# S5 responses beside the q, k, v products, S5 input tables beside the output projection, memory keys and values kept in SBUF

## The reference, cut to what matters

```python
for i in range(DEPTH):
    h = rms_norm(x, norm_w[i])
    if i % 2 == 0: seq_out, z, xq = gla_branch(h, ...)      # q, k, v, r, z, xq = h @ w_in
    else:          seq_out, z, xq = s5_branch(h, ...)       # x_t = Ab x_{t-1} + Bb u_t ; y_t = Re(C x_t)
    xa = memory_attention(xq, mem_n, xa_w_kv[i])
    x = x + (concatenate([seq_out, xa]) * silu(z)) @ w_out[i]
```

## Time and profile before

| | |
|---|---|
| median of 3 runs | 3059.97 us (3059.89 to 3063.43) |
| the profiled execution, its time | 3060.32 us |
| its span on the core | 3058.5 us |
| PE busy | 2840.8 us (93%) |
| DVE, ACT, POOL busy | 1407.5, 997.1, 1110.8 us |
| mean granted TensorE clock | 0.971 of full speed |
| DMA | 324.88 MB, mean 106 GB/s |

### The profile page before, as it was taken

The page is one execution under the profiler, slowest core; times in us unless marked ns, Lnnn a source line. Parts: engine busy times, 40 slices in busy tenths (PEclk is TensorE's granted clock), DMA queues, the critical chain, the costliest instruction groups (busy, mean ns, idle before and its releaser), DMA issues.

```text
span 3058.5 us, 45007 instructions
## 1 busy us (share of the span) xinstructions
PE 2840.8 (93%) x17982; PEld 2335.4 (76%) x17982; DVE 1407.5 (46%) x2200; ACT 997.1 (33%) x1525; POOL 1110.8 (36%) x780
## 2 busy tenths in 40 slices
PE   7998889899999999899989888899998999899997
PEld 5676567678788578787768877899997877678885
DVE  7688364510206611402138675570634456382452
ACT  2222444222312235523225333412124455332211
POOL 1332022444233179443433423244442321244442
PEclk9999999999999999999999998999999998999999
DMA  5888111145573279322221100222222210122222
GB/s 182 248 266 257 58 42 49 63 153 158 158 216 103 97 176 257 112 96 90 90 88 64 43 3 23 70 90 90 91 91 75 81 45 22 56 89 96 91 95 76
DMA packets 130815, 324.88 MB, mean 106 GB/s; under 512 B 54144, under 2 KB 54784, under 8 KB 129872
## 3 DMA queue, kind: packets, MB, share of 16 engines
q1 hardware_dynamic: 96272, 222.95, 22.8%
q0 software_dynamic: 30016, 87.92, 10.2%
q10 hardware_dynamic: 4352, 11.50, 1.0%
HBM read 288.32 MB, written 33.95 MB: 105 GB/s over the span
## 4 chain that ended last, share of the span: by engine, by line
PE 70%; DVE 16%; ACT 4%; DMA 3%; issue 3%; POOL 3%; DVEq 1%; ACTq 0%; SPq 0%; POOLq 0%
PE ps L270 17%; PE ps L273 17%; PE ps L275 17%; DMA d_pb<-arena 3%; POOL ring_r L363 2%; PE ps L280 2%; PE ps L925 1%; PE ps L1876 1%; PE ps L1615 1%; ACT high L372 1%; DVE h L603 1%; PE ps L1707 1%; PE ps L2291 1%; PE ps L3003 1%; DVE x L600 1%
## 5 line engine op out<-in xcount | busy, mean ns | idle before, releaser
L363 POOL TENSOR_TENSOR ring_r<-ring,high 128x1024 fp32r<-128x1024 f32 x335 | 834.4, 2491 | 1388.7 <-ACT high L372 1388.7
L270 PE MATMUL ps<-h_hi,high 128*128 128x512 f32 (+1 forms) x2104 | 735.4, 358 | 46.1 <-POOL ring_r L363 27.2
L275 PE MATMUL ps<-h_hi,ring_r 128*128 128x512 f32 (+1 forms) x2104 | 661.6, 349 | 0.0
L372 ACT ACTIVATE high<-ring 128x1024 fp32r<-128x1024 f32 x367 | 387.8, 1057 | 831.1 <-PE ps L270 695.7
L273 PE MATMUL ps<-h_r,high 128*128 128x512 f32 (+1 forms) x1912 | 642.9, 346 | 0.0
L270 PEld LDWEIGHTS ps<-h_hi,high 128*128 128x128 f32 x2104 | 400.1, 190 | 120.9 <-issue 48.3
L275 PEld LDWEIGHTS ps<-h_hi,ring_r 128*128 128x128 f32 x2104 | 370.0, 190 | 53.8
L273 PEld LDWEIGHTS ps<-h_r,high 128*128 128x128 f32 x1912 | 364.2, 190 | 41.9 <-issue 1.4
L273 PE MATMUL ps<-f_r,high 128*128 128x264 f32 (+1 forms) x960 | 295.1, 321 | 0.0
L270 PE MATMUL ps<-f_hi,high 128*128 128x264 f32 (+1 forms) x896 | 270.9, 317 | 2.2 <-POOL ring_r L363 1.7
L275 PE MATMUL ps<-f_hi,ring_r 128*128 128x264 f32 (+1 forms) x896 | 230.8, 316 | 0.0
(11 more groups left out here) (489 smaller groups left out, 4254.6 us busy)
## 6 DMA issues: line engine op xcount, KB each, us to landing
ring<-in_units SPq DMA_DIRECT2D x402, 512.0 KB, 3.3
d_ca<-arena POOLq DMA_DIRECT2D x16, 640.0 KB, 9.1
arena<-d_ca POOLq DMA_DIRECT2D x16, 640.0 KB, 6.0
arena<-d_q POOLq DMA_DIRECT2D x32, 256.0 KB, 8.0
d_pb<-arena POOLq DMA_DIRECT2D x16, 512.0 KB, 11.2
arena<-d_pb POOLq DMA_DIRECT2D x16, 512.0 KB, 4.0
arena<-d_ca POOLq DMA_DIRECT2D x16, 512.0 KB, 5.2
arena<-d_k POOLq DMA_DIRECT2D x128, 64.0 KB, 4.3
```

The lines of the kernel that those rows point to most:

```text
L270: part = mm(acc, hi[:, cols], self.x_hi(k)[:, t0:t0 + tn], start=(k == 0), stop=False)
L275: ins = mm(acc, w[:, cols], self.x_hi(k)[:, t0:t0 + tn], start=False, stop=(k == self.kt - 1))
L363: eng.tensor_tensor(b.ring_r[:, slot, :], b.ring[:, slot, :], self.high[:, (j + self.flip) % 2, :], ALU.subtract).then_inc(b.unit_lo, 1)
L372: b.nc.scalar.activation(self.high[:, (j + self.flip) % 2, :], b.ring[:, u % RING, :], ACT.Copy).then_inc(b.unit_hi, 1)
```

## The change

What each edit does:

- In xq, q, k, v, PE computes the responses of block n right after the second of the block's two units (`unit_tensor`, `respond`), from the `ca` in SBUF: 8 products with 32 weight columns (16 lag columns that nobody uses, and the 16 of Bb), each group written to one of four bands of 32 PSUM partitions. ACT keeps them (`keep_response`) after the high part of the unit two later, POOL stores them by 4 DMAs a block. POOL now loads only `cin` and `bin` for a block, stores 128 of the 160 columns of `ca`, and no `pb`. DVE makes no `pb` there. The loops over xq, q, k, v are written out.
- In `out0`, `S5InputTables` takes the place of `S5Responses`: DVE makes `pb` for two blocks ahead of each tile's add, POOL issues for each block a load of `bk` (512 KB), two loads of powers (`d_q`, 256 KB each) and a store of `pb` (512 KB). PE has only the projection.
- The memory's keys and values stay in SBUF; their two stores and two loads are gone.
- The norm of layer 1 also waits until the `pb` stores have landed; the next memory keys wait for nothing of the responses.

```diff
@@ S5Tables @@
+    def respond(self, pe, n):
+        b, m, par = self.b, self.m, n % 2
+        pe.wait_ge(self.made, n + 1)
+        if n >= 2:
+            pe.wait_ge(self.k_kept, n - 1)
+        for g in range(8):
+            i, j = divmod(g, QUARTERS)
+            ins = b.nc.tensor.matmul(b.ps[32 * j:32 * j + 32, 4 + 2 * par, i * P:(i + 1) * P],
+                                     m.ca[par][:, g, P:P + 32], m.ca[par][:, g, 0:P], start=True, stop=True)
+        ins.then_inc(self.responded, 1)
...
             if not isinstance(it, int) or it > 0:
-                dve.wait_ge(self.block_out[par], it * 32)
+                dve.wait_ge(self.block_out[par], it * 16)
+                dve.wait_ge(self.responded, m_ - 1)
...
-            inner(tt(bb, bb, small, ALU.add))
-            q, k = m.qk[par], m.bk[par]
-            t512 = m.tmp[:, 0:512]
...
-            inner(tt(t512, q[:, 1], k[0], ALU.mult))
-            tt(pbv[:, 1], pbv[:, 1], eight(t512), ALU.add).then_inc(self.made, 1)
+            tt(bb, bb, small, ALU.add).then_inc(self.made, 1)
@@ class S5InputTables(Stage) @@
+        def load(n):
+            par = n % 2
+            pool.dma_start(m.bk[par], a["s5_bk"][n].unsqueeze(0).broadcast_to([S5_C, S5_H, 2, 512])
+                           ).then_inc(self.block_in[par], 16)
+            q = b.d_q.rearrange("c k (m n) -> m k c n", m=NB)[n]
+            for c in range(2):
+                pool.dma_start(m.qk[par][:, c], q[:, c].unsqueeze(1).broadcast_to([S5_C, S5_H, 512])
+                               ).then_inc(self.block_in[par], 16)
...
+        def store(n):
+            pool.wait_ge(self.made, NB + n + 1)
+            pool.dma_start(b.d_pb[n], m.pb_made[n % 2]).then_inc(self.stored[n % 2], 16)
 
         load(0)
         load(1)
         for o in range(KD):
             for u in range(3 * o + 1, 3 * o + 4):
                 gemm.low_unit(pool, u)
                 if u == 3 * o + 1 and o:
                     for n in (2 * o - 2, 2 * o - 1):
                         store(n)
                         load(n + 2)
...
+    def scalar(self, act):
+        for o in range(KD):
+            for u in range(3 * o + 1, 3 * o + 4):
+                gemm.high_unit(act, u)
+            gemm.out_scalar(act, o)
...
+    def vector(self, dve):
+        b, gemm = self.b, self.beside
+        for o in range(KD):
+            self.block(dve, 2 * o)
+            self.block(dve, 2 * o + 1)
+            it, i = divmod(o, gemm.body_outs)
+            par, full = gemm.count(i, it)
+            dve.wait_ge(b.filled[par], full)
+            gemm.store("dve", o, gemm.bank(o), o).then_inc(b.stored[par], 1)
+            if o >= 2:
+                self.norm.add(dve, o - 1)
...
-        stages.append(LoadMemory())
+        stages.append(S5LastResponse(tables))
```

More of the change, by code:

```diff
@@ L178, in loop @@
     def loop(self, eng, body):
-        if self.squared_by or self.high is None and self.then or self.high is not None and (self.iters == 2 or self.after or self.before):
+        if self.aside or self.squared_by or self.high is None and self.then or self.high is not None and (self.iters == 2 or self.after or self.before):
             for it in range(self.iters):
@@ L1291, in __init__ @@
         self.beside = []
-        self.done = [(self.block_out[c], 32 * NB // 2) for c in range(2)]
+        self.cleared = b.sem("s5t_cleared")
+        self.responded = b.sem("s5t_responded")
+        self.k_kept = b.sem("s5t_k_kept")
+        self.k_stored = [b.sem("s5t_k_even"), b.sem("s5t_k_odd")]
+        self.done = [(self.block_out[c], 16 * NB // 2) for c in range(2)]
+        self.done += [(self.k_stored[c], 16 * QUARTERS * NB // 2) for c in range(2)]
     def load(self, pool, m_, par):
@@ L1298, in load @@
         pool.dma_start(m.bin[par], a["s5_ba"][m_]).then_inc(s, 16)
[L1299 to L1304, removed]
+    LOADS, INNER = 2, 5
     def store_powers(self, pool):
@@ L1602, in tensor @@
     def tensor(self, pe):
[L1603 to L1617 removed]
+        for o in range(KD):
+            self.beside.out_tensor(pe, o)
@@ L3457, in build @@
         m0.state = view(30848, 3, DV)
-        m0.rank = m0.state[:, 2, :]
+        m0.rank = view(24064, L1)
         m0.att = view(32384, 2, P)
@@ L3617, in build @@
         rms.follow(g)
+        s5b = S5InputTables(b, m5, a, g, rms, [gla.done, (tables.q_stored, 16)], tables)
+        rms.needs = out0_done + s5b.done
+        stages.append(s5b)
         stages.append(rms)
         km1 = view(30848, KD, N_MEM)
-        def keep_first(which, m, parts, o):
-            if m == 0:
-                for sem, v in s5r.done:
-                    nc.scalar.wait_ge(sem, v)
-            return copy(which, km1[:, m, :], parts[0])
-        first_keys = Gemm(b, "mem_k1a", "fm", memn, KD, KD // 2, MEMS, keep_first, A, [(s5r.k_kept, NB)], first_bank=4)
+        first_keys = Gemm(b, "mem_k1a", "fm", memn, KD, KD // 2, MEMS, keep(km1), A, [], first_bank=4)
         stages.append(first_keys)
```

197 lines of the change are left out of this document (92 added, 105 removed).

## The result

| | before | changed |
|---|---|---|
| median of the runs, us | 3059.93 (3054.62 to 3063.43) | 3113.45 (3105.34 to 3122.69) |
| span of the profiled execution, us | 3058.5 | 3103.3 |
| q, k, v: first rank product starts, us | 304.20 | 282.86 |
| output projection: adds of tile 0 and 7, us | 624.46, 768.52 | 603.11, 816.69 |

The ratio is 1.018 (95% interval 1.014 to 1.021). I had forecast 3095 us: the sign was right and the time too low, and two large errors of opposite sign lie under that. (The profiled execution of the changed kernel was the fastest of its four, 3105.34 us.) The q, k, v stretch came out 21.3 us shorter where I had it 0.8 longer, and the seven tiles from the first to the last add took 213.6 us where I had 176.4.

What follows compares the result with a forecast made beforehand. It took PE to bound q, k, v after the change, and a closed loop through the loads to bound the output projection. Against 3060.3 us, 0.8 + 36.4 - 2.5 = +34.7 gave 3095 us; own range 3086 to 3110.

Steps and rivals of the forecast that it cites:

- The q, k, v stretch: xq, q, k, v products: PE becomes the bound, products 179.0 us plus responses 32 us, so the stretch ends 0.8 us later.
- the term for the responses: PE in q, k, v: eight response products with switches cost 2.0 us a block, 32 us for 16 blocks.
- all four bands at once: Lower bound for a block's responses on PE in q, k, v: 1.8/4 + 0.2 = 0.65 us.
- the loop: Output projection: no load is issued ahead, one tile is one closed loop of 25.2 us, +36.4 us in all.
- the burst: Output projection: stores and loads from POOL's first issue until the second block can start, taken as 16.0 us a tile.
- longer loop: Rival, output projection: burst 19.2 us with weights, or POOL's issues delay a remainder; tile 28.4 us, 3117 us; chance 0.13.
- my own sum of 17.9: Burst in the projection: 11.5 us from the trace, plus 2.5 for added stores and 3.9 for added loads at 202 GB/s.
- The first tile: Output projection: two blocks (8.4 us) precede its add, which comes at 628.5 us, before at 624.46.
- The keys and values: Memory's keys and values kept in SBUF: 0, since their reads lay under 13.85 us of rank products on PE.
- The tail: Behind the last add: next keys start 3.6 us sooner, the norm waits for the last store; taken as -2.5 us.
- Parallel bands: Rival, q, k, v: responses overlap twofold, 1.1 us a block, stretch 14.4 us shorter, 3081 us; chance 0.30.
- Loads at the stores' rate: Rival, output projection: broadcast loads flow at 417 GB/s, a tile takes 17.8 us, 3043 us; chance 0.10.

Runs made afterwards that it cites:

- Experiment 1: Changed kernel with all eight response products of a block on one band of 32 columns instead of four: 3134.54 us.
- experiment 4: Changed kernel with the input tables' loads, blocks and stores left out of the output projection: 3009.28 us.
- experiment 7: Changed kernel with a tile's two stores and six loads issued by POOL ahead of the remainder of unit 3o+1 instead of behind it: 3047.89 us.
- experiment 6: Changed kernel with only the loads of q taken from rows that no partitions share, B's load as it is: 3097.16 us.
- Experiment 9: Changed kernel with 20 of the projection's 24 weight units copied a second time by SyncE into memory that nothing reads: 3132.10 us.
- experiment 5: Changed kernel with the loads of both B and q taken from rows of another table that no partitions share: 3068.02 us.
- experiment 10: Built on experiment 3: even blocks' input tables beside q, k, v, odd blocks' beside the output projection, one a tile: 3032.61 us.
- experiment 11: As experiment 10, with even blocks' loads one POOL turn earlier and a semaphore of its own for the table store: 3016.05 us.
- experiment 3: Kernel before with only the responses moved beside q, k, v in four bands, their stores at the head of POOL's turn: 3030.82 us.
- experiment 8: Changed kernel with B and q loads from unshared rows, and a tile's stores and loads issued ahead of the remainder: 3032.40 us.

## Why the prediction was wrong

**The q, k, v stretch: the term for the responses was mis-sized.** The mechanism was right: DVE falls under PE, the store wait goes, PE is the bound. The start moved up by more than I had (92.22 for the first xq product instead of 94.0). The step that failed is "I take 2.0, the form nearest in the rows". It measured 0.67, at the bound that I had written down for all four bands at once. Experiment 1 puts one band at 1.3 us a block more, and the end of the stretch moves by 16 times that. A small part of the 2.0 was mine as well: I had 0.2 for the switches, while the earlier trace rows have 3.92 - 0.23 - 3.60 = 0.09 for two blocks, and 0.1 came. The old products went to one band, so their row could not bear on how several bands behave; I let it decide because it was the only row. 16 x 1.33 = 21.3 us.

**The output projection: the loop was right, the burst mis-sized.** The loop's order, its waits and its small parts were as put (experiments 4 and 7 show that it is the cause). The step that failed is "I take 16.0": the burst measured 21.6 in the mean of seven. The tile of my own "longer loop", 28.4 us, was still under the 30.5 that came. What the runs show of the 5.6 us:

- I took the burst 1.9 us under my own sum of 17.9, in the hope that B's 4 KB rows flow faster. They don't (experiment 6).
- My sum had one weight unit in it. The whole burst lies in one stretch, and a stage that uses three units a tile fetches three while it lasts: a burst moves 4.7 MB, not 3.67. Experiment 9 prices a unit at 1.45 us, so two are 2.9.
- The remaining 0.8 no run places, and it may be more: the 11.5 us that my sum started from held 2.35 MB in the trace of before, 0.44 of it an older store that the new burst doesn't have, worth 1.1 us at the stores' rate. A lower rate of the shared loads would fill the gap. The 202 GB/s of the earlier trace rows had some weights mixed in; where hardly anything but shared loads seems to flow, from 649 to 653 us, it is

```profile
DMA packets 204, 0.73 MB, mean 183 GB/s; under 512 B 25, under 2 KB 25, under 8 KB 204
```

  which would make 2.10 MB of them 11.5 us instead of 10.4. This part was not tried by itself.

As a mean over the burst, the rate that I had used was fair: 4.7 MB in 21.6 us are 219 GB/s, my sum has, by its own count, 3.67 MB in 17.9 us, 205. In the main it was the bytes that were wrong. Seven tiles of 30.5 instead of 25.2 are 37 us.

**The first tile: mis-sized, and hidden.** I let it cost 4.0 us, since two blocks stand before its add. From the first rank product to the add lie 320.2 us, 320.3 before, so it seems to have cost nothing. But PE begins the tile's last product at 600.36 and DVE adds at 603.11, 2.75 us later; before it was 0.44 (624.02 and 624.46). So the add is 2.3 us later behind PE. DVE's rows show what it still had to do:

```profile
592.65 0.69 DVE L1689 TENSOR_TENSOR arena<-h 128x512 f32<-128x512 f32 x1
...
597.02 2.55 DVE L1688 TENSOR_TENSOR arena<-h 128x512 f32<-128x512 f32 x1 [0.90 <-DMA h<-d_q]
...
603.11 0.69 DVE L3621 TENSOR_TENSOR x<-x,ps 128x512 f32<-128x512 f32 x1
```

What hid it is the stretch ahead, which I had put at no change. It varies by more than that: experiment 1 has the changed kernel's instructions from the first rank product to the first add and takes 331.7 us, 11.5 more, with a granted clock of 0.88 instead of 0.95 in the 70 us that start 47 us behind that product. Why it varies is open, and a part of every difference of a few microseconds between two kernels here may be this.

**The keys and values: 0, neither shown nor refuted.** From the first rank product to the first add the kernels that leave them in SBUF take 320 to 332 us, those that send them through DRAM 318 to 323. Two kernels with the same instructions there lie 11.5 apart, and no run moved the keys and values alone.

**The tail: not as put, and its size can't be read.** I had the next keys start 3.6 us sooner behind the last add. They start 4.6 us behind it instead of 5.3, 0.7 sooner, since PE first waits for DVE's squares:

```profile
818.12 2.05 PE L580 MATMUL ps<-sq,c_ones 128*128 128x512 f32 x2 [12.68 <-DVE sq L543]
821.30 13.98 PE L283 MATMUL ps<-memn,ring 128*128 128x256 f32 x64
```

The first product of u is 0.7 us sooner too. Of the profiled difference of 44.8, after -21.3 and +69.5, -3.4 is left, near my -2.5. But that is all of the launch behind the last add, which takes 2285 to 2293 us in the kernels built on the changed one; the agreement is luck.

**The rivals.** "Parallel bands" came, with all four and not twofold. "A longer loop" came as well, by the first of its two ways and beyond its price; I had held them apart, and my range had no place for both together, though their effects, -21 and +37, partly cancel. The 3113 us that came lie past the forecast's own range (3086 to 3110); that they still lie in the 3066 to 3114 drawn around the rivals is luck, two errors against each other. "Loads at the stores' rate" did not come: own rows were needed for that (experiment 5), and even then a tile was 24.3, because the loop's order cost as much as its rate. The row was the right one to follow. The Trainium skill's price for a DMA ("DMA: Bandwidth & Descriptors", Anatomy of one DMA) is nearer to loads of rows of their own (422 GB/s in experiment 5) than to shared ones (183). By it the burst of my sum is 2.0 + 8.4 = 10.4 us, an estimate, not the "about 9" that I wrote.

## What to carry to other kernels

When work is moved beside another stage, write down all bytes that must flow between the event that starts its loads and the instruction that needs them, the other queues' included, and then ask whether the start can be issued one step earlier: here that one question was worth 66 us (experiment 7). A stage has room for some of a job where it has none for all of it; splitting the tables over two stages left both bound by TensorE, once the loads and stores stood early enough in the queue (experiments 10 and 11). Where two edits lie on one shared queue, the order of issue decides: two lines in POOL's turn were worth 28 us at a DMA share that even rose (experiment 3).

## What the runs showed of the hardware

- Four bands of 32 columns: eight products of two passes take 0.57 us spread over the bands, 1.87 us on one, 3.3-fold.
- Loads in which many partitions read the same rows flow at 183 to 213 GB/s with all engines full (649 to 653 us of the changed kernel, and the earlier trace rows); with rows of their own at 416 and 422 (experiment 5), like the stores at 417. In the burst the same loads land in 7.3 and 8.0 us instead of 9.7 and 13.1. Rows of 4 KB shared by 8 partitions and rows of 2 KB shared by 16 cost the same for their bytes.
- A two-input DVE instruction that starts inside POOL's two-input instruction ends only behind it, 2.4 to 2.9 us instead of 0.69. The Trainium skill has this as a lock ("SBUF — State Buffer", SBUF: two separate sides: whichever of the two starts first holds the shared port pair for its whole instruction); the trace of experiment 8 agrees, in all 11 cases from 639 to 740 us.
